# Two-layer hybrid decoder on one core: low halves of split weights written over the raw units in the weight ring

## The reference

```python
for layer in range(DEPTH):                       # DEPTH = 2
    hn = rms_norm(h, norm_mix[layer])
    h = h + hybrid_mixer(hn, w_in[layer], ..., w_branch[layer], w_out[layer], cos, sin)
    hn = rms_norm(h, norm_ffn[layer])
    if layer % 2 == 0:
        h = h + swiglu(hn, dense_w_gate[i], dense_w_up[i], dense_w_down[i])
    else:
        h = h + moe_swiglu(hn, router[i], moe_w_gate[i], moe_w_up[i], moe_w_down[i])
return rms_norm(h, final_norm)
```

## Time and profile before

| | before |
|---|---|
| median of 3 runs | 1725.57 us (1725.4 to 1725.92) |
| span of the profiled execution | 1724.4 us |
| its own time beside the span | not given; the median run is 1.2 us above the span |
| PE, DVE, ACT busy | 91%, 70%, 50% of the span |
| PE's mean granted clock | 0.947 |
| HBM traffic | 383 MB, 223 GB/s over the span |

### The profile page before, as it was taken

How to read it: one execution, slowest core, us unless ns; L and a number is a source line. 1 busy time by engine, 2 the same in 40 slices (tenths; PEclk the granted TensorE clock), 3 DMA queues, 4 the chain that set the end, 5 groups by cost and what they waited for, 6 DMA issues and landing times.

```text
span 1724.4 us, 25996 instructions
## 1 busy us (share of the span) xinstructions
PE 1567.3 (91%) x10143; PEld 1430.6 (83%) x10143; DVE 1212.7 (70%) x1226; ACT 856.2 (50%) x752; POOL 65.1 (4%) x43
## 2 busy tenths in 40 slices
PE   5989898699996889898599999999999999999995
PEld 5878777699986778777599898998989989899894
DVE  4874634555545874544578888888888888888885
ACT  3423232343423323242267676675767767677672
POOL 0111000000001112000000000000000000000000
PEclk8989999799997989999599999999999999999998
DMA  6323153855402323241979899998999989899880
GB/s 213 128 92 123 49 196 118 297 191 178 145 1 93 127 78 128 78 156 49 343 261 350 292 362 329 308 359 270 361 308 331 361 279 358 300 341 362 283 281 26
DMA packets 267333, 383.98 MB, mean 223 GB/s; under 512 B 9344, under 2 KB 212480, under 8 KB 267136
## 3 DMA queue, kind: packets, MB, share of 16 engines
q1 hardware_dynamic: 267120, 382.50, 65.9%
q10 hardware_dynamic: 144, 0.52, 0.1%
HBM read 381.95 MB, written 1.05 MB: 222 GB/s over the span
## 4 chain that ended last, share of the span: by engine, by line
PE 82%; DVE 8%; issue 4%; ACT 3%; DMA 1%; POOL 1%; SPq 0%; DVEq 0%; ACTq 0%; POOLq 0%
PE ps L469 24%; PE ps L470 24%; PE ps L471 23%; ACT w_hi L1035 2%; PE ps L608 1%; PE ps L625 1%; DVE m_lo L1252 1%; PE ps L621 1%; PE ps L812 1%; PE ps L800 1%; DVE w_lo L1526 1%; PE ps L799 1%; DVE qkvT L1307 1%; PE ps L506 1%; ACT m_hi L928 1%
## 5 line engine op out<-in xcount | busy, mean ns | idle before, releaser
L1526 DVE TENSOR_TENSOR w_lo<-ring,w_hi 128x2048 fp32r<-128x2048 f32 x297 | 680.1, 2290 | 133.6 <-ACT w_hi L1035 133.4
L1035 ACT ACTIVATE w_hi<-ring 128x2048 fp32r<-128x2048 f32 x297 | 569.1, 1917 | 169.5 <-PE ps L471 149.1
L469 PE MATMUL ps<-w_hi,xg_hi 128*128 128x256 f32 x1408 | 406.4, 289 | 7.0 <-ACT gselT L1074 5.0
L470 PE MATMUL ps<-w_lo,xg_hi 128*128 128x256 f32 x1408 | 399.0, 283 | 0.0
L471 PE MATMUL ps<-w_hi,xg_lo 128*128 128x256 f32 x1408 | 398.7, 283 | 0.0
L469 PEld LDWEIGHTS ps<-w_hi,xg_hi 128*128 128x128 f32 x1408 | 270.2, 192 | 13.8 <-issue 10.3
L470 PEld LDWEIGHTS ps<-w_lo,xg_hi 128*128 128x128 f32 x1408 | 270.6, 192 | 3.0
L471 PEld LDWEIGHTS ps<-w_hi,xg_lo 128*128 128x128 f32 x1408 | 270.6, 192 | 0.0
L1252 DVE TENSOR_TENSOR m_lo<-ring,m_hi 128x2048 fp32r<-128x2048 f32 x64 | 145.8, 2289 | 162.5 <-ACT m_hi L928 162.2
L928 ACT ACTIVATE m_hi<-ring 128x2048 fp32r<-128x2048 f32 x64 | 121.7, 1911 | 135.9 <-PE ps L471 127.6
L469 PE MATMUL ps<-w_hi,actT_hi 128*128 128x512 f32 x352 | 140.0, 398 | 17.8 <-DVE actT_lo L1577 17.8
(11 more groups left out here) (270 smaller groups left out, 2270.8 us busy)
## 6 DMA issues: line engine op xcount, KB each, us to landing
ring<-in_moe_w_gate_dram SPq DMA_DIRECT2D x88, 1024.0 KB, 5.7
ring<-in_moe_w_up_dram SPq DMA_DIRECT2D x88, 1024.0 KB, 6.1
ring<-in_moe_w_down_dram SPq DMA_DIRECT2D x88, 1024.0 KB, 5.3
ring<-in_w_in_dram SPq DMA_DIRECT2D x48, 1024.0 KB, 5.2
ring<-in_dense_w_gate_dram SPq DMA_DIRECT2D x11, 1024.0 KB, 5.4
ring<-in_dense_w_up_dram SPq DMA_DIRECT2D x11, 1024.0 KB, 6.4
ring<-in_dense_w_down_dram SPq DMA_DIRECT2D x11, 1024.0 KB, 5.0
ring<-in_w_branch_dram SPq DMA_DIRECT2D x8, 1024.0 KB, 4.9
```

The lines of the kernel that those rows point to most:

```text
L469: mm(dst, xh, yh, start=start, stop=False)
L470: mm(dst, xh, yl, start=False, stop=False)
L1035: go(split_of(j)[0], ring[:, j % SLOTS, :], ACT.Copy).then_inc(hi_ready, 1)
L1526: tt(wl, ring[:, j % SLOTS, :], wh.bitcast(f32), ALU.subtract).then_inc(lo_ready, 1)
```

## The change

Three things, all in the buffers of the split weights.

1. The low half is written over the raw unit, in the ring slot where it lies. `ring_lo` is the ring's memory under another type, and `w_lo` and `m_lo` are gone. DVE no longer waits for PE before it makes a low half.
2. A ring slot is free for the next load only when PE is done with its unit: the loads wait on `unit_used` in place of `lo_ready`.
3. In the mixers the nine slots that were three raw, three high, three low are five for raw and low together, and four for high. The high copy of unit i waits for unit i - 4 of this mixer; the first four of the second mixer wait for nothing but the end of the network before.

The networks keep three high buffers.

```diff
 SPLITS = 3
-MIX_SLOTS = 3
+MIX_SLOTS = 5
+MIX_HIGH = 4
...
         ring = sb("ring", SLOTS, UNIT)
+        ring_lo = nc.alloc_sbuf_tensor_at("ring_lo", [P, SLOTS, UNIT], f32r, offset=ring_at)
...
-        w_lo = phase("w_lo", f32r, SPLITS, UNIT)
...
-        m_hi = phase("m_hi", f32r, SPLITS, UNIT, at=ring_at + 4 * UNIT * MIX_SLOTS)
-        m_lo = phase("m_lo", f32r, SPLITS, UNIT, at=ring_at + 4 * UNIT * (MIX_SLOTS + SPLITS))
...
+        m_hi = phase("m_hi", f32r, MIX_HIGH, UNIT, at=ring_at + 4 * UNIT * MIX_SLOTS)
...
-            return w_hi[:, j % SPLITS, :], w_lo[:, j % SPLITS, :]
+            return w_hi[:, j % SPLITS, :], ring_lo[:, j % SLOTS, :]
...
                 if before is not None:
-                    sp.wait_ge(lo_ready, before + 1)
+                    sp.wait_ge(unit_used, before + 1)
...
-                        sp.wait_ge(lo_ready, e * PASS_UNITS + (i - SLOTS + 1))
+                        sp.wait_ge(unit_used, e * PASS_UNITS + (i - SLOTS + 1))
...
                         act.wait_ge(loaded[slot], value)
-                        if i >= SPLITS:
-                            act.wait_ge(unit_used, i - SPLITS + 1)
-                        if n_split[0] < SPLITS and base:
+                        if n_split[0] >= MIX_HIGH:
+                            act.wait_ge(unit_used, i - MIX_HIGH + 1)
+                        elif base:
                             act.wait_ge(unit_used, base)
...
                         dve.wait_ge(hi_ready, i + 1)
-                        if i >= SPLITS:
-                            dve.wait_ge(unit_used, i - SPLITS + 1)
-                        if n_split[0] < SPLITS and base:
-                            dve.wait_ge(unit_used, base)
-                        b = n_split[0] % SPLITS
-                        tt(m_lo[:, b, :], ring[:, plan[i][0], :], m_hi[:, b, :].bitcast(f32),
+                        slot = plan[i][0]
+                        tt(ring_lo[:, slot, :], ring[:, slot, :], m_hi[:, n_split[0] % MIX_HIGH, :].bitcast(f32),
                            ALU.subtract).then_inc(lo_ready, 1)
...
                 dve.wait_ge(hi_ready, off + (j + 1))
-                dve.wait_ge(unit_used, off + (j - SPLITS + 1))
```

More of the change, by code:

```diff
@@ L195, in build @@
         assert max(dense_end, place[0]) <= nc.sbuf_usable_end
-        m_hi = phase("m_hi", f32r, SPLITS, UNIT, at=ring_at + 4 * UNIT * MIX_SLOTS)
-        m_lo = phase("m_lo", f32r, SPLITS, UNIT, at=ring_at + 4 * UNIT * (MIX_SLOTS + SPLITS))
-        mx_hi = phase("mx_hi", f32r, KD, SEQ, at=ring_at + 4 * UNIT * (MIX_SLOTS + 2 * SPLITS))
-        mx_lo = phase("mx_lo", f32r, KD, SEQ, at=ring_at + 4 * UNIT * (MIX_SLOTS + 2 * SPLITS + 1))
-        assert MIX_SLOTS + 2 * SPLITS + 2 <= SLOTS and KD * SEQ == UNIT
+        m_hi = phase("m_hi", f32r, MIX_HIGH, UNIT, at=ring_at + 4 * UNIT * MIX_SLOTS)
+        mx_hi = phase("mx_hi", f32r, KD, SEQ, at=ring_at + 4 * UNIT * (MIX_SLOTS + MIX_HIGH))
+        mx_lo = phase("mx_lo", f32r, KD, SEQ, at=ring_at + 4 * UNIT * (MIX_SLOTS + MIX_HIGH + 1))
+        assert MIX_SLOTS + MIX_HIGH + 2 <= SLOTS and KD * SEQ == UNIT
         br_hi = phase("br_hi", f32r, 2, H, SEQ, at=rT_at)
@@ L347, in mixer_split @@
         def mixer_split(n, k):
-            return tuple(m[:, n % SPLITS, :].rearrange("p (k n) -> p k n", k=k) for m in (m_hi, m_lo))
+            return tuple(m.rearrange("p (k n) -> p k n", k=k)
+                         for m in (m_hi[:, n % MIX_HIGH, :], ring_lo[:, n % MIX_SLOTS, :]))
         def w_in_units(layer, col):
@@ L923, in split_upto @@
                         act.wait_ge(loaded[slot], value)
-                        if i >= SPLITS:
-                            act.wait_ge(unit_used, i - SPLITS + 1)
-                        if n_split[0] < SPLITS and base:
+                        if n_split[0] >= MIX_HIGH:
+                            act.wait_ge(unit_used, i - MIX_HIGH + 1)
+                        elif base:
                             act.wait_ge(unit_used, base)
-                        go(m_hi[:, n_split[0] % SPLITS, :], ring[:, slot, :], ACT.Copy).then_inc(hi_ready, 1)
+                        go(m_hi[:, n_split[0] % MIX_HIGH, :], ring[:, slot, :], ACT.Copy).then_inc(hi_ready, 1)
                         n_split[0] += 1
```

## The result

| | before | after |
|---|---|---|
| median of 6 runs, us | 1725.49 (1724.79 to 1726.53) | 1719.33 (1718.98 to 1721.41) |
| ratio, 95% interval | | 0.9965 (0.9954 to 0.9977) |
| profiled execution, span, us | 1724.4 | 1717.1 |

The median is 6.2 us lower, 0.36%; the two profiled executions differ by 7.3 us.

A forecast was written before the change was run, and what follows sets the result against it. PE was taken as the bound, so only its waits and clock could give time. 1.05 us per mixer, 2.1 in both, half kept because of the clock: 1725.57 - 1.05 = 1724.5 us, range 1720.8 to 1727.9.

The forecast's parts named there:

- The step that failed: Dense network: PE busy 189.96 of 190.20 us, so nothing to win there; time comes only from PE's waits and clock.
- a difference in stretches without any clock change: Whole span: a sign that would show the forecast wrong, the span differing from before where the clock did not change.
- Fourth high buffer: Mixers' convolution: unit 3's high copy comes early, PE's wait before it goes; 1.05 us per mixer, 2.1 in both.
- Half the gain kept because of the clock: Mixers: between 2.1 us kept and 0, depending on PE's clock; half taken, 1.05 us.
- clock against it: Rival, mixers: PE's 2.0 us wait brings half clock and the first mixer's step takes 2.26 us more; 1727.3 us, chance 0.21.
- favourable one: Rival, mixers: 2.1 us kept and the second mixer's stretch 2.26 us shorter, like the first's; 1721.2 us, chance 0.24.
- The loads wait for PE: Mixers, first dense units, experts: later loads cost nothing, with 4, 4 and 15 us of cover.
- later units have more room: Mixers: loads after unit 5's, which has 4 us of cover, have more time before ACT wants them.
- Writing in place: DVE's low halves: no extra time, zero taken, from in-place steps of 1.23 us against 1.22.
- slow one: Two rivals: experts' loads come late, 1748.8 us, chance 0.04; in-place halves slow on DVE, 1789 us, chance 0.02.

The follow-up runs named there:

- b2: Kernel before, with the networks' low-half buffer moved by 32 bytes and all buffers behind it by 128, nothing in place: 1721.91 us, ratio 0.9983.
- a3: Changed kernel with low halves in place in the dense network and experts only, mixers 3/3/3 as before: 1722.46 us, ratio 0.9982.
- a4: Changed kernel with the change in the mixers only; the networks keep their separate low buffers and old load waits: 1725.72 us, ratio 0.9999.
- b4: Changed kernel with 32 bytes left free ahead of the ring and 96 behind it: 1720.54 us, ratio 0.9963.
- c1: Changed kernel with the networks' high weights at the ring's start address modulo 512 bytes and the inputs 96 bytes off it: 1719.35 us, ratio 0.9958.
- d3: Changed kernel with the experts' stationary low halves 96 bytes off their high halves, modulo 512: 1719.45 us, ratio 0.9959.
- d4: Changed kernel with only the experts' high buffers at the ring's start address modulo 512 bytes, in a second tile: 1717.57 us, ratio 0.9952.
- d5: The changed kernel itself, timed again beside other kernels: 1719.49 us, ratio 0.9962.
- a6: Changed kernel with three high buffers in the mixers for four: 1723.73 us, ratio 0.9985.
- a1: Changed kernel with the old low buffers' 24 KB left empty, so later buffers lie where they lay before: 1719.98 us, ratio 0.9967.
- c3: Kernel before, with the networks' inputs 96 bytes further on and both weight halves left in place: 1725.99 us, ratio 1.0.
- c2: Changed kernel with the networks' high weights and inputs all at the ring's start address modulo 512 bytes: 1721.96 us, ratio 0.9975.
- d2: Kernel before, with the mixers' low halves 96 bytes off their high halves modulo 512, all behind them 512 on: 1725.57 us, ratio 0.9997.

## Why the forecast was wrong

- **The step that failed** is in the first paragraph: the dense network has PE busy 189.96 of 190.20 us, "nothing to win in either". A busy PE was read as a fixed time. The busy time was itself made longer by how the operands lay: 1320 matmuls went from 189.96 to 187.42 us with no wait removed. For writing in place the forecast asked only what it costs DVE ("I take zero"); it also moved an operand of PE, and b2 shows the new pace with that operand moved by 32 bytes and nothing else but the buffers behind it. The forecast named the sign of this itself, a difference in stretches without any clock change, and had no case for it. The network part alone (a3) is worth 3.5 us against the median beside it (interval 1 to 5); its other half, the experts, the forecast took for bound by PE in the same way.
- *Fourth high buffer.* Its mechanism held: unit 3 at 29.64 (forecast 29.6), no wait before unit 3, 1.90 us before unit 5 (forecast 2.0). Convolution 0 at 46.78 in place of the forecast 46.4, convolution 1 at 59.73 in place of 59.4, the products at 68.40 in place of 68.1: 0.75 us for 1.05. The high copy of unit 4 began at 42.62, not 42.2, and so DVE was the later by 0.4.
- *Half the gain kept because of the clock, 1.05 us.* This size is not settled. In a4, which has this part alone, the median did not move (1725.72 beside 1725.94), and its interval, about 1.7 us either way, holds both 0 and the 1.05. In the changed kernel the step from the products to L589 is 25.68 us in the first mixer and 25.69 in the second, where it was 24.03 and 26.29. So the first went most of the way that the "clock against it" rival has for it (1.65 of 2.26 us), and the second only a quarter of the way that the favourable one has (0.6 of 2.26). The mixers' 0.77 us lost and 1.92 won lie within what kernels with one and the same mixers show, and do not measure it.
- *The loads wait for PE, cost nothing.* Held: with the loads late (a3, after) ACT waits for no load inside a pass, and the experts' landings are 5.4 to 5.8 us. The one long wait, for the first expert's first unit, stands in the kernel before too (25.7 us after, 20.3 before), ahead of the routing. In the mixers, "later units have more room" did not hold: in six profiles with five raw slots (a4, b4, c1, d3, d4, d5) a load ends ACT's idle time ahead of one copy of `w_out` at some 780 us, 3.7 to 4.1 us of it. In after PE ends the same idle time, 3.70 us, so the load and PE come within tenths of each other. It cost nothing that shows: the second mixer is 301.72 us in d5 and 301.66 in after.
- *Writing in place, cost nothing.* Held in the networks, 2290 ns for each of 297 low halves; in the mixers the mean of the page's second row is 2354 ns, where it was 2289. Five of the 64 halves make the whole difference. The last two rows, of the timeline, show the longest:

```profile
L1522 DVE TENSOR_TENSOR ring_lo<-ring,w_hi 128x2048 fp32r<-128x2048 f32 x297 | 680.1, 2290 | 128.0 <-ACT w_hi L1036 128.0
...
L1249 DVE TENSOR_TENSOR ring_lo<-ring,m_hi 128x2048 fp32r<-128x2048 f32 x64 | 150.0, 2354 | 108.9 <-ACT m_hi L929 108.6
```

```profile
542.33 1.90 POOL L1171 TENSOR_TENSOR work<-cst,sm 128x1024 f32<-128x1024 f32 x1 [19.98 <-DVE sm L1292]
542.37 4.01 DVE L1249 TENSOR_TENSOR ring_lo<-ring,m_hi 128x2048 fp32r<-128x2048 f32 x1
```

  Unit 3's half in the second mixer, now made early, fell beside a step of POOL and took 4.01 us; the other four (2.41 us twice, 3.40 twice) stand beside POOL steps as well, and a6, with three high buffers, has none of the five. The Trainium skill ("SBUF — State Buffer", section "SBUF: two separate sides") says that DVE, in an instruction with two inputs in SBUF, and GpSimd share one pair of ports, which one holds alone for its whole instruction; this row agrees, 1.7 us more beside a POOL step of 1.90. It cost PE nothing: from there to the products at 577.03 PE's one wait for a low half is that before unit 5, 1.90 us as in the first mixer.
- *Rivals.* Neither slow one came: no lead was too short, DVE was not the bound. The favourable clock (1721.2) came nearest to the time, for the wrong reason. No rival had the pace of PE in it.

## What to carry over

Where PE is busy without a gap, look at the time from one matmul's start to the next before calling the stretch fixed: a mean of 120 ns for 256 columns at full clock was here the sign that the halves of the weights began at one remainder. An edit that moves a buffer moves that too, and a control that only shifts the buffer by 32 or 96 bytes tells it from the edit's own effect. A small gain in front of a stretch that hangs on the clock can come out as nothing (a4) or as 2.5 to 4.4 us (a3 and a6 against after, a1 and d5), so a part is best measured in the kernel that it will live in. And a stage of one profile is compared with the same stage of kernels that did not change it, before its difference is called a gain.

## What was not expected of the hardware

In these kernels the spacing of the products of split halves depends on how their buffers' start addresses stand to each other. With one remainder for the two halves of the stationary weights, the dense network's 256-column products took 119.8 to 120.0 ns, wherever the inputs lay (c1, c3); 32, 96 or 192 bytes apart they took 117.8 to 117.9, and 128 apart 119.1. The 512-column products follow another order: they are quickest where weights and activations begin at one remainder (227.8 ns in c2) and slowest where both halves lie 96 bytes from the activations (233.4 to 233.6). At half clock there is nothing of it: from about 327 us on the products follow at 213 to 214 ns both before and after, which is 256 columns at 1.2 GHz. At full clock 256 columns would be 106.7 ns, so each product takes 11 to 13 ns more than that, and only there.

Which part of the chip makes this, no run here tells. Nor is the rule complete: 96 bytes gave 2.0 ns in the dense network and 0.9 in the mixers' convolution (d2), where the units are read in the same form. Other differences than 32, 96, 128 and 192 bytes were not tried, and that 512 is the right number to take the remainder of was not tested.
